# First attention's end: nine dependent steps for the head weights, coefficients repeated and turned, and spreads placed inside the first pair of the output projection

## The reference, cut to what matters

```python
for (window, dilation), n_g in zip(ATTN_PATTERNS, HEAD_GROUPS):
    o_g, lse_g = dilated_window_attention(q[:, :, sl], k[:, :, sl], v[:, :, sl], window, dilation)
    outs.append(o_g)
    lses.append(jax.nn.logsumexp(lse_g, axis=-1) - math.log(n_g))
alpha = jax.nn.softmax(jnp.stack(lses, axis=-1), axis=-1)
merged = jnp.concatenate(
    [o_g * (N_ATTN_GROUPS * alpha[:, :, g]).astype(o_g.dtype)[:, :, None, None] for g, o_g in enumerate(outs)],
    axis=2).reshape(B, S, D_ATTN)
return jnp.einsum('bse,ed->bsd', merged, w_out)
```

## Time and profile before

| | us |
|---|---|
| median of 3 runs | 3209.9 |
| the profiled execution, its own time | 3216.56 |
| its span in the profile | 3214.9 |
| TensorE busy | 3081.5 |
| VectorE busy | 1752.3 |
| ScalarE busy | 1199.2 |

### The profile page before, as it was taken

How to read it: one execution, slowest core, us unless ns; L and a number is a source line. 1 busy time by engine, 2 the same in 40 slices (tenths; PEclk the granted TensorE clock), 3 DMA queues, 4 the chain that set the end, 5 groups by cost and what they waited for, 6 DMA issues and landing times.

```text
span 3214.9 us, 39389 instructions
## 1 busy us (share of the span) xinstructions
PE 3081.5 (96%) x14295; PEld 2536.7 (79%) x14295; DVE 1752.3 (55%) x2784; ACT 1199.2 (37%) x1703; POOL 125.3 (4%) x117
## 2 busy tenths in 40 slices
PE   7899999988999999999898999999999999899998
PEld 5788888876888878888786788888888877678887
DVE  6677524755776356643676666424332566753323
ACT  3423323464323244432334544324442334544422
POOL 0000000000000000000030000000000002000000
PEclk8999999988999999999998999999999999899999
DMA  3355333202554336532320355322333322023332
GB/s 116 115 186 185 111 98 94 92 27 79 183 189 145 98 105 200 172 101 93 82 84 30 108 187 193 101 94 84 97 98 98 96 72 72 27 86 98 97 100 77
DMA packets 262906, 351.31 MB, mean 109 GB/s; under 512 B 16664, under 2 KB 208536, under 8 KB 262808
## 3 DMA queue, kind: packets, MB, share of 16 engines
q1 hardware_dynamic: 240768, 270.57, 27.0%
q0 software_dynamic: 21360, 79.01, 7.5%
q10 hardware_dynamic: 680, 0.43, 0.0%
HBM read 348.75 MB, written 2.10 MB: 109 GB/s over the span
## 4 chain that ended last, share of the span: by engine, by line
PE 88%; DVE 6%; ACT 3%; issue 2%; DMA 0%; SPq 0%; DVEq 0%; ACTq 0%
PE bank L1728 28%; PE bank L1730 28%; PE bank L1729 28%; DVE w_lo L1030 1%; ACT w_hi L612 1%; DVE sumsq L1043 1%; PE bank L1992 1%; DVE work L1083 1%; PE bank L2066 0%; DVE h_lo L1089 0%; ACT probs L902 0%; PE bank L2124 0%; PE bank L1769 0%; DMA raw<-in_pool_w_in_dram 0%; DVE xT L1094 0%
## 5 line engine op out<-in xcount | busy, mean ns | idle before, releaser
L1030 DVE TENSOR_TENSOR w_lo<-raw,w_hi 128x1024 fp32r<-128x1024 f32 x482 | 589.6, 1224 | 1197.1 <-ACT w_hi L612 1196.5
L1728 PE MATMUL bank<-h_hi,w_hi 128*128 128x512 f32 x2864 | 1137.7, 397 | 21.4 <-DVE h_lo L1089 8.8
L1730 PE MATMUL bank<-h_hi,w_lo 128*128 128x512 f32 x2864 | 1125.3, 393 | 0.0
L1729 PE MATMUL bank<-h_lo,w_hi 128*128 128x512 f32 x2864 | 1125.1, 393 | 0.0
L612 ACT ACTIVATE w_hi<-raw 128x1024 fp32r<-128x1024 f32 x508 | 538.1, 1059 | 1383.2 <-PE bank L1730 1378.6
L1728 PEld LDWEIGHTS bank<-h_hi,w_hi 128*128 128x128 f32 x2864 | 544.3, 190 | 141.9 <-issue 25.2
L1730 PEld LDWEIGHTS bank<-h_hi,w_lo 128*128 128x128 f32 x2864 | 543.8, 190 | 116.2
L1729 PEld LDWEIGHTS bank<-h_lo,w_hi 128*128 128x128 f32 x2864 | 544.8, 190 | 109.0
L1728 PE MATMUL bank<-act_hi,w_hi 128*128 (+1 forms) x1120 | 435.9, 389 | 1.0 <-DVE w_lo L1030 1.0
L1730 PE MATMUL bank<-act_hi,w_lo 128*128 (+1 forms) x1120 | 435.7, 389 | 0.0
L1729 PE MATMUL bank<-act_lo,w_hi 128*128 (+1 forms) x1120 | 435.7, 389 | 0.0
(11 more groups left out here) (294 smaller groups left out, 2376.6 us busy)
## 6 DMA issues: line engine op xcount, KB each, us to landing
raw<-in_ffn_w_in_dram SPq DMA_DIRECT2D x176, 512.0 KB, 3.5
ada_w<-in_ada_w_dram POOLq DMA_DIRECT2D x72, 1024.0 KB, 5.5
raw<-in_ffn_w_out_dram SPq DMA_DIRECT2D x88, 512.0 KB, 3.6
raw<-in_ffn_w_gate_dram SPq DMA_DIRECT2D x44, 512.0 KB, 3.8
raw<-in_ffn_w_up_dram SPq DMA_DIRECT2D x44, 512.0 KB, 3.8
raw<-in_ffn_w_down_dram SPq DMA_DIRECT2D x44, 512.0 KB, 3.8
raw<-in_mix_w_in_dram SPq DMA_DIRECT2D x44, 512.0 KB, 3.6
raw<-in_attn_w_qkv_dram SPq DMA_DIRECT2D x24, 512.0 KB, 3.6
```

Source lines behind the costliest of these rows:

```text
L1030: V.tensor_tensor(w_lo[:, nb % SPL, :], raw[:, nb % RAW, :], w_hi[:, nb % SPL, :].bitcast(F32), ALU.subtract).then_inc(s_lo, 1)
L1728: T.matmul(dst, wh, mh, start=first, stop=False)
L1729: T.matmul(dst, wh, ml, start=False, stop=False)
L1730: return T.matmul(dst, wl, mh, start=False, stop=last)
```

## The change

It does five things. The head weights are computed in fewer steps: the factors 1/n and 3 are folded into a constant row (`small`, 16 more columns) and into a third of den, the reciprocals are taken earlier, the three group sums are not linked with each other. The sums are turned right after the last step's transposes, before the values of head 14, and back before those of head 15. The selection matrix, `cTh` and `cTl` are gone: `repeat_coefs` on ScalarE writes the coefficients of two heads 64 times along the free dimension (128x512, into `work`'s slots 2 and 3), and four transposes on TensorE (`spread_pair`) turn this into the spread. Twelve filler matmuls stand before the first spread. Spreads 0 to 3 stand before the output projection, spreads 4 to 7 inside its first half pair, one behind the matmuls of chunk 0, 1, 2 and 3 each. And `o_out` of heads 6 to 15 runs over the tokens in order: it writes `oT` contiguously and reads the PSUM bank at a distance of 128 elements, where before it read contiguously and wrote every fourth element.

```diff
+for lo, hi in HEAD_GROUPS:
+    small[:, 67 + lo:67 + hi] = len(HEAD_GROUPS) / (hi - lo)
...
+SPREAD_BANKS = (6, 7, 4, 5)
...
-                dst, src = by_class(dst), classes(src)
+                dst, src = dst.rearrange("p (j r) -> p j r", r=4), src.rearrange("p (r j) -> p j r", r=4)
             nc.scalar.activation(dst, src, ACT.Copy).then_inc(s_o, 1)
+
+        def repeat_coefs(n):
+
+            if n == 0:
+                act.wait_ge(s_on, 1)
+            if n >= 2:
+                act.wait_ge(s_otr, n - 1)
+            nc.scalar.activation(work[:, 2 + n % 2, :].rearrange("p (b h d) -> p b h d", h=2, d=HD),
+                                 a1["fine"][:, 5, :, 2 * n:2 * n + 2].unsqueeze(3).to_broadcast([P, NB, 2, HD]), ACT.Copy)\
+                .then_inc(s_coefs0, 1)
...
-        o_out(nh - 2)
         act.wait_ge(s_sumT, 1)
         nc.scalar.activation(b_["sumsT"][0:20, :], bank[7][0:20, :], ACT.Copy).then_inc(s_sumA, 1)
+        o_out(nh - 2)
         act.wait_ge(s_aw, 1)
         nc.scalar.activation(a1["fine"][:, 1], a1["fine"][:, 0], ACT.Exp).then_inc(s_ae, 1)
         o_out(nh - 1)
-        act.wait_ge(s_otr, 1)
-        nc.scalar.activation(b_["cTh"][0:nh, :], bank[6][0:nh, :], ACT.Copy).then_inc(s_ch, 1)
-        for n in range(nh // 2):
-            act.wait_ge(s_on, n + 2)
-            nc.scalar.activation(a1["out_hi"][:, n, :], work[:, n % 2, :], ACT.Copy).then_inc(s_hhi, 1)
+        for n in range(nh // 2 + 2):
+            if n < nh // 2:
+                repeat_coefs(n)
+            if n >= 2:
+                c = n - 2
+                act.wait_ge(s_on, c + 2)
+                nc.scalar.activation(a1["out_hi"][:, c, :], work[:, c % 2, :], ACT.Copy).then_inc(s_hhi, 1)
...
-        nmx, den = F[:, 6], F[:, 7]
+        share, coef, nmx, den = F[:, 2], F[:, 5], F[:, 6], F[:, 7]
+        least, ex, wsum, tot = F[:, 4, :, 1:2], F[:, 1], F[:, 3, :, 0:3], F[:, 4, :, 0:1]
+        third = 1.0 / len(HEAD_GROUPS)
+        here, there = slice(0, DILATED), slice(DILATED, 16)
+
+        def own(n):
+            return bufs["sums"][:, 24 * n:24 * n + 24].rearrange("p (h b) -> p b h", b=NB)
+
+        def back(n):
+            return bank[1][:, 0:20 * NB].rearrange("p (b h) -> p b h", h=20)[:, :, 10 * n:10 * n + 10]
+
         dve.wait_ge(s_exp, n_steps)
-        for n, dst in enumerate((nmx, den)):
-            V.tensor_copy(dst[:, :, 0:DILATED], bufs["sums"][:, 24 * n:24 * n + 24].rearrange("p (h b) -> p b h", b=NB))
+        V.tensor_copy(nmx[:, :, here], own(0))
+        link(V.tensor_scalar(den[:, :, here], own(1), third, None, ALU.mult))
+        V.reciprocal(coef[:, :, here], den[:, :, here])
         dve.wait_ge(s_sumB, 1)
-        for n, dst in enumerate((nmx, den)):
-            back = bank[1][:, 0:20 * NB].rearrange("p (b h) -> p b h", h=20)[:, :, 10 * n:10 * n + 10]
-            ins = V.tensor_copy(dst[:, :, DILATED:16], back)
-        link(ins)
-        least, ex, wsum, tot = F[:, 2, :, 0:1], F[:, 1], F[:, 3, :, 0:3], F[:, 4, :, 0:1]
+        link(V.tensor_copy(nmx[:, :, there], back(0)))
         link(V.tensor_reduce(least, nmx, AX_X, ALU.min))
-
         V.tensor_tensor(F[:, 0], least.to_broadcast([P, NB, 16]), nmx, ALU.subtract).then_inc(s_aw, 1)
+        link(V.tensor_scalar(den[:, :, there], back(1), third, None, ALU.mult))
+        V.tensor_tensor(share, den, small[:, 67:83].unsqueeze(1).to_broadcast([P, NB, 16]), ALU.mult)
+        link(V.reciprocal(coef[:, :, there], den[:, :, there]))
         dve.wait_ge(s_ae, 1)
-        link(V.tensor_tensor(ex, ex, den, ALU.mult))
+        link(V.tensor_tensor(ex, ex, share, ALU.mult))
         for g, (lo, hi) in enumerate(HEAD_GROUPS):
-            link(V.tensor_reduce(F[:, 3, :, g:g + 1], ex[:, :, lo:hi], AX_X, ALU.add))
-            link(V.tensor_scalar(F[:, 3, :, g:g + 1], F[:, 3, :, g:g + 1], 1.0 / (hi - lo), None, ALU.mult))
+            last = V.tensor_reduce(F[:, 3, :, g:g + 1], ex[:, :, lo:hi], AX_X, ALU.add)
+        link(last)
         link(V.tensor_reduce(tot, wsum, AX_X, ALU.add))
         link(V.reciprocal(tot, tot))
-        link(V.tensor_scalar(tot, tot, float(len(HEAD_GROUPS)), None, ALU.mult))
         link(V.tensor_tensor(wsum, wsum, tot.to_broadcast([P, NB, 3]), ALU.mult))
-        link(V.reciprocal(F[:, 5], den))
         for g, (lo, hi) in enumerate(HEAD_GROUPS):
-            last = V.tensor_tensor(F[:, 5, :, lo:hi], F[:, 5, :, lo:hi],
+            last = V.tensor_tensor(coef[:, :, lo:hi], coef[:, :, lo:hi],
                                    F[:, 3, :, g:g + 1].to_broadcast([P, NB, hi - lo]), ALU.mult)
         last.then_inc(s_on, 1)
-        dve.wait_ge(s_ch, 1)
-        V.tensor_tensor(bufs["cTl"][0:nh, :], bank[6][0:nh, :], bufs["cTh"][0:nh, :].bitcast(F32), ALU.subtract).then_inc(s_cl, 1)
-        dve.wait_ge(s_o, nh)
         base = H0["attn0"]
         for n in range(nh // 2 + 1):
             if n < nh // 2:
-                dve.wait_ge(s_otr, n + 2)
+                dve.wait_ge(s_otr, n + 1)
+                dve.wait_ge(s_o, 2 * n + 2)
                 if n >= 2:
                     dve.wait_ge(s_hlo, base + n - 1)
-                V.tensor_tensor(work[:, n % 2, :], bufs["oT"][:, n, :], bank[7 - n % 2][:], ALU.mult).then_inc(s_on, 1)
+                V.tensor_tensor(work[:, n % 2, :], bufs["oT"][:, n, :], bank[SPREAD_BANKS[n % 4]][:], ALU.mult)\
+                    .then_inc(s_on, 1)
...
+            if between is not None and c == 1 and k < KC - 1:
+                between(k)
...
+            if s == n_steps - 1:
+                for r in range(4):
+                    ins = T.transpose(bank[7][0:20, r::4], bufs["sums"][:, 48 + r::4], ident)
+                ins.then_inc(s_sumT, 1)
...
-        for r in range(4):
-            ins = T.transpose(bank[7][0:20, r::4], bufs["sums"][:, 48 + r::4], ident)
-        ins.then_inc(s_sumT, 1)
-        values(nh - 1)
         pe.wait_ge(s_sumA, 1)
         for b in range(NB):
             ins = T.transpose(bank[1][:, 20 * b:20 * b + 20], bufs["sumsT"][0:20, b * P:(b + 1) * P], ident[0:20, 0:20])
         ins.then_inc(s_sumB, 1)
-
-        pe.wait_ge(s_on, 1)
+        values(nh - 1)
+        keep_warm(12, 0)
+        for n in range(4):
+            spread_pair(n)
+
+    def spread_pair(n):
+
+        pe.wait_ge(s_coefs0, n + 1)
+        if n < 4:
+            pe.wait_ge(s_o, (13, 13, 15, 16)[n])
+        else:
+            pe.wait_ge(s_on, n - 4 + 2)
         for b in range(NB):
-            ins = T.transpose(bank[6][0:nh, b * P:(b + 1) * P], bufs["fine"][:, 5, b, 0:nh], ident)
+            ins = T.transpose(bank[SPREAD_BANKS[n % 4]][:, b * P:(b + 1) * P], work[:, 2 + n % 2, b * P:(b + 1) * P], ident)
         ins.then_inc(s_otr, 1)
-        pe.wait_ge(s_sel, 1)
-        pe.wait_ge(s_cl, 1)
-        for n in range(nh // 2):
-            if n >= 2:
-                pe.wait_ge(s_on, n)
-            pick = sel[0:nh, 2 * n:2 * n + 2, :].rearrange("p h d -> p (h d)")
-            T.matmul(bank[7 - n % 2][:], pick, bufs["cTh"][0:nh, :], start=True, stop=False)
-            T.matmul(bank[7 - n % 2][:], pick, bufs["cTl"][0:nh, :], start=False, stop=True).then_inc(s_otr, 1)
...
+              lambda k: spread_pair(4 + k) if k < 4 else None)
```

39 lines of the change are left out of this document (19 added, 20 removed).

## The result

| | us |
|---|---|
| before, median of 5 runs on this chip (lowest to highest) | 3209.9 (3209.07 to 3214.94) |
| changed, median of 5 runs (lowest to highest) | 3192.33 (3190.56 to 3197.6) |
| ratio, 95% interval | 0.9947 (0.9936 to 0.9959) |
| the changed kernel's profiled execution, its own time | 3192.33 |
| its span in the profile | 3190.7 |

The change takes 17.6 us off the median; by the ratio's interval it is 13 to 21 us. The profiled execution is the median run itself; that of before stood 6.66 above its own median.

What follows compares the result with a forecast made beforehand. TensorE was taken to bound the kernel (busy 3081.5 of 3214.9 us), with ScalarE deciding the steps of heads 6 to 15. End -9.3 plus layout -3.3 gave -12.6: 3209.9 to 3197.3 us, range 3194.0 to 3203.0.

Steps and rivals of the forecast that it cites:

- rival 1: Output layout: the strided PSUM read costs what the strided write did, only the end counts, 3200.6 us; chance 0.32.
- Seven outputs by 0.48: Loop steps: seven of eight strided outputs on the path get 0.48 us shorter each, -3.3 us; bounds 0 and -4.
- the coefficients 2.4 earlier: Last step's end: chain starts 1.2 us earlier and is 1.2 shorter, so coefficients are ready at 734.3 instead of 736.73.
- where I had 1.2: VectorE's coefficient chain: fewer linked steps, a smaller reciprocal and folded factors shorten it, sum -1.2 us.
- I said 1.5: Coefficients to first product: one repeat on ScalarE and a pack of four transposes, 1.5 us instead of 3.86.
- 10.7 + 2.4 = 13.1: Projection's first pair: 48 matmuls at full clock take 10.7 us, the four packs inside add 2.4.
- I take 1.8 of loss: End: TensorE's clock may fall in gaps before the packs, costing 1.0 to 3.4 us; 1.8 assumed.
- -9.3: The end's whole term: all-warm gain of -11.1 us less 1.8 of clock loss; bounds -7.7 and -11.1.
- my bound of -11.1: The end, all warm: projection starts 10.4 us earlier, packs add 2.4, matmuls at full clock save 3.1.
- I take that offset as unchanged: Sum: the profile lies 6.7 us above the runs, and the same offset is assumed after the change.
- Rival 2: End: clock stays at 0.50 through the last pack and following matmuls, end worth -0.4, 3209.5 or 3206.2 us; chance 0.09.
- Rival 3: Output layout: the strided read is far dearer than the strided write, up to +17 us, 3217.6 us; chance 0.03.

Runs made afterwards that it cites:

- the second run with fillers at the start: Changed kernel plus 20 filler matmuls in TensorE's pause ahead of the attention's first scores, measured again on another chip: 3190.76 us, ratio 0.994.
- two of my runs: Kernel before with only the new o_out layout: 3206.13 us, ratio 0.9983; changed kernel with the old o_out layout: 3198.73 us, ratio 0.9951.
- the run with fillers at the start: Changed kernel plus 20 filler matmuls in TensorE's pause ahead of the attention's first scores, first measurement: 3187.51 us, ratio 0.9932.
- the second execution of before: Kernel before with nothing changed, profiled once more because its first profile stood high: 3208.15 us.
- alone in the old end: Kernel before plus 38 filler matmuls in TensorE's wait for the coefficients, nothing else changed: 3208.66 us, ratio 0.9996.

## Why the prediction came out as it did

**The layout's mechanism was right.** The outputs take 590 ns; I had taken 0.59 and given rival 1 (the strided read as dear as the strided write) 0.32. Rival 1 falls. The Trainium skill ("PSUM — Partial Sum Buffer", Specifications) says that any non-contiguous access slows matmuls significantly. It speaks of matmuls; carried over to ScalarE's reads of PSUM, 512 bytes apart, the rule doesn't hold: 589/590/593 ns for all 16, six of which (heads 0 to 5) read contiguously. On the write side the Trainium skill ("Advanced Engine Details and Errata", SBUF Cachelines) gives SBUF lines of 16 bytes and a penalty when each access takes another line; every fourth 4-byte element is that case, and the trace agrees (1062 to 1103 ns for the ten strided outputs of before against 588 to 592 for its six contiguous ones).

**Its size: two errors that nearly cancel.** Seven outputs by 0.48 was 3.3; start to start a step gains 0.38 to 0.49, in all 2.93. My seven were the loop's eight less one in the stretch at 0.50, and that reason was wrong: the eighth counts too, but it stands in the last step, and what it costs shows in the end. I counted the loop only; the end holds 0.94 that my sum didn't have. Where it lies is seen with the old layout, in its second profile, where the last step starts at 720.32:

```profile
722.29 1.08 ACT L897 ACTIVATE a_oT<-bank 64x512 f32<-64x512 f32 x1
723.39 0.60 ACT L889 ACTIVATE a_probsT_hi<-bank 128x512 fp32r<-128x512 f32 x1
723.89 0.57 ACT L926 ACTIVATE a_sums_turned<-bank 20x512 f32<-20x512 f32 x1
...
725.67 0.20 DVE L1610 COPY a_fine<-bank 128x40 f32<-128x40 f32 x1 [0.44 <-PE bank L2186]
```

The sums' copy starts 3.57 behind the last step's start, against 720.51 - 717.40 = 3.11 in the changed kernel: the eighth output stands in front of it. That is 0.46 for the output itself. VectorE has the turned-back sums 1.78 behind the copy's start, against 1.26: TensorE, at 0.50 from 718.9 to 725.7 there and at 1.00 in the changed kernel, comes later from head 14's values. This 0.52 goes with the clock: in the second run with fillers at the start, which has the new layout, the clock was at 0.50 in the last step too, and the coefficients came 0.63 later (7.99 against 7.36) without any strided output. So the layout was worth 3.4 by its own time and 3.9 with the clock, where I took 3.3.

Whether the layout also moves the clock, which was the rival of two of my runs, is not settled, but the profiles lean that way: in all six with the strided output the clock was at 0.50 somewhere between step 14 and the last step's sums, in the eight with the contiguous one only once.

**The chain.** I had the coefficients 2.4 earlier. With the old layout, the state in which I worked that out, they are 10.84 - 8.30 = 2.54 earlier; the new order alone is 1.46 where I had 1.2. From the coefficients to the first product 1.41 (I said 1.5), to the projection 3.75 (I said 4.1, the fourth pack waits 0.58 for ScalarE as foreseen).

**The overlap.** The first pair with its four packs takes 13.11 from its first matmul, where I had 10.7 + 2.4 = 13.1. That this fits so well is luck: with all spreads first the pair alone takes 11.24 at a clock of 1.00, so the packs cost 1.87. My 10.7 was too low, because the 35 matmuls of 7.80 us include some that only reach into the stretch (the rows of the pair add up to 50, and it has 48), and my 2.4 was too high. Without the interleaving the end is 3.17 longer. TensorE isn't starved by packs 4 to 7, and the slab's splits aren't late.

**The step that failed: "I take 1.8 of loss".** The clock was 1.00 from 678 to past 741.6. Nothing was lost, where my sum gave up 1.8. I had the bounds right (1.0 to 3.4 if it falls) but took a fall as the likely case, because it fell at 713.7 behind a stretch with TensorE 4.68 of 6.80 busy. The changed kernel has 4.66 of 6.70 at 710.7 to 717.4 and the clock holds. The runs with the old chain and without fillers show that a fall there is not far off: in their profiles it came, and cost 1.75 and 0.63.

**The sum, for the execution it was made against.** The end went from 36.99 to 24.22, -12.77, against -9.3: 1.8 for the clock, 0.94 for the layout in the end, 0.35 from the coefficients to the projection, 0.14 for the chain, 0.24 for a pair that had taken 14.05 where I had 13.8 (3.5 together). This is beyond my bound of -11.1 by 1.7, of which the layout's share in the end is the larger half. In steps 14 to 21 -4.33 against -3.3.

**"I take that offset as unchanged".** It went from 6.66 to nothing: the profiled execution fell by 24.2, the median by 17.6. The stretches at 0.50 that I read as the kernel's were partly that one execution's. Against the second one, whose time is 1.7 below the median, the end gave 11.29 and the steps 2.93, 14.2 in all. Of the 3.4 that remain to 17.6, 1.7 is that execution's place below its median, and 1.6 lies ahead of the attention, where nothing was changed. So of the 5.0 by which I missed, 1.6 lie where the change is: 2.0 more in the end (the 3.5 above, less the 1.48 by which before's own end is shorter in its second execution) and 0.4 less in the steps. The other 3.4 lie between executions and, as far as the anchors show, are luck and not the change. Even by this fairer reading the end beats my bound of 11.1, by 0.2.

**Rival 2** (the clock stays low through the first matmuls) falls with the row of 1.00. The Trainium skill ("TensorE: Matmul & The Clock Gate", Part 4) says that the full clock doesn't engage for transposes; here it held through stretches of transposes and waits alone: from 724.8 to 728.5 in the changed kernel (2.24 of 3.70 busy, 1.00), and from 724.7 to 732.8 with all spreads first (4.81 of 8.10 busy, 1.00). That is a clock which stays, not one which rises. Without fillers and with the old chain it was at 0.50 through the packs, or the later ones, and rose only behind the projection's first matmuls, which the rule allows. So what speaks against the rule here is the clock that stayed.

**Rival 3** (a dearer read) falls by the 590 ns.

**What stays open.** Ahead of the first step 666.2 to 668.5, and behind the pair's end 2446.0 to 2452.0, the programs of all these runs are the same or nearly so, and their spans move by up to 6 us. It isn't a constant of a kernel: before has shown both 2449.0 and 2452.0. I made no run on it, but the traces show where it comes from. Set against each other by the starts of ScalarE's `w_hi`, two executions run alike for long and then part in jumps. Two of these jumps, looked at closely, lie where the granted clock differs. Behind the pair's end, the run with fillers at the start gains 1.61 us on the changed kernel between 798 and 807 us (counted in the changed kernel), where the same part of the program reads, first in the changed kernel, then in that run:

```profile
800.80:804.20 3.40, 3.40 (x9) 2.62 (x9) 3.31 (x6) 1.23 (x2) 0.00 (x0) 0.50 0.98 357
...
797.90:801.30 3.40, 3.40 (x17) 2.81 (x16) 3.30 (x6) 1.24 (x2) 0.00 (x0) 1.00 0.97 360
```

And ahead of the attention, the second execution of before loses 1.6 us to the changed kernel near 172, first before, then changed:

```profile
171.40:174.80 3.40, 3.40 (x8) 2.75 (x9) 3.40 (x5) 0.52 (x1) 0.00 (x0) 0.50 0.89 338
...
169.80:173.20 3.40, 3.38 (x15) 2.79 (x16) 3.40 (x5) 0.47 (x1) 0.00 (x0) 1.00 0.92 348
```

So at least these jumps are stretches at 0.50 that one execution has and the other hasn't. What decides in which execution they come isn't known. Differences of medians below some 3 us are therefore not given to any edit above; the anchors are.

## What to carry to other kernels

Where a copy has to reorder, let it read PSUM with the stride and write SBUF contiguously, and price it from the start of the instruction behind it, not from its own duration. Where a pause of TensorE lies in front of dense work, shorten it first, and try fillers then. What they gave differed from place to place, with what stands behind the pause: 0.3 us alone in the old end, 0.6 in the new one, 1.1 to 3.2 ahead of the first scores. Before a clock stretch goes into a sum, take a second execution; its place and length differed here between two executions of one program, by 2.8 us in a single step.
